# The output projection and the plain feed-forward in one block, at two stage borders

## What is computed

```
def squared_relu_mlp(h, w_up, w_down):
    return jnp.square(jax.nn.relu(h @ w_up)) @ w_down
...
        if layer % 2 == 0:
            x = x + gdn_shortconv_mixer(h, ev_w_in[i], ev_qkv_conv[i], ev_a_log[i], ev_dt_bias[i],
                                        ev_o_norm[i], ev_sc_conv[i], ev_w_out[i])
        else:
            x = x + nsa_mixer(h, od_w_in[i], od_cmp_pos[i], od_cmp_k_w1[i], od_cmp_k_w2[i],
                              od_cmp_v_w1[i], od_cmp_v_w2[i], od_w_out[i])
        x = x + squared_relu_mlp(rms_norm_2(x, mlp_norm[layer]), w_up[layer], w_down[layer])
    return rms_norm_2(x, final_norm)
```

## Time and profile before

| | us |
|---|---|
| median of 3 runs | 2354.27 |
| lowest, highest | 2346.55, 2355.38 |
| profiled execution | 2354.56 |
| its span | 2352.8 |
| TensorE busy | 2245.4 |
| VectorE busy | 986.6 |
| ScalarE busy | 752.9 |
| GpSimd busy | 193.3 |

### The profile page before, as it was taken

One profiled execution on the slowest core, in us unless ns is written; L12 is line 12 of the kernel. 1 busy time (PEld: TensorE's weight loads), 2 busy tenths in 40 slices (PEclk: granted clock), 3 DMA queues, 4 the chain that ended last, 5 costly groups with the idle time before them and its releaser, 6 DMA issues. The chain is left out here.

```text
span 2352.8 us, 30416 instructions
## 1 busy us (share of the span) xinstructions
PE 2245.4 (95%) x12790; PEld 1689.8 (72%) x12790; DVE 986.6 (42%) x1683; ACT 752.9 (32%) x1241; POOL 193.3 (8%) x214
## 2 busy tenths in 40 slices
PE   7999999889999999999999999999998999999997
PEld 4746555768888877874667888887875667888885
DVE  4123366443332334856344433423347653432433
ACT  3233211222222223444133322422125653331331
POOL 1004100000000000022000000000225540000000
PEclk9999999799999998999999999998999999999999
DMA  7240022212223112201031222213410012222210
GB/s 322 98 180 36 1 73 99 83 72 76 86 90 126 63 54 101 107 1 73 19 126 72 82 98 108 99 48 110 143 41 32 2 41 77 99 108 98 82 72 36
DMA packets 17110, 195.83 MB, mean 83 GB/s; under 512 B 2000, under 2 KB 3152, under 8 KB 5072
## 3 DMA queue, kind: packets, MB, share of 16 engines
q1 hardware_dynamic: 15824, 189.67, 21.7%
q10 hardware_dynamic: 1152, 4.23, 0.4%
HBM read 189.70 MB, written 2.10 MB: 82 GB/s over the span
## 5 line engine op out<-in xcount | busy, mean ns | idle before, releaser
L1733 DVE TENSOR_TENSOR wsp_mlp<-ring,wsp_mlp 128x1024 fp32r<-128x1024 f32 x128 | 156.8, 1225 | 438.0 <-ACT wsp_mlp L1695 438.0
L1695 ACT CAST wsp_mlp<-ring 128x1024 fp32r<-128x1024 f32 x128 | 134.3, 1049 | 349.2 <-PE psum L1680 344.8
L1677 PE MATMUL psum<-hs_mlp,wsp_mlp 128*128 128x512 f32 x512 | 201.7, 394 | 8.1 <-DVE hs_mlp L1566 8.1
L1677 PE MATMUL psum<-acts_mlp,wsp_mlp 128*128 128x512 f32 x512 | 202.4, 395 | 0.0
L1679 PE MATMUL psum<-hs_mlp,wsp_mlp 128*128 128x512 f32 x512 | 201.1, 393 | 0.0
L1680 PE MATMUL psum<-hs_mlp,wsp_mlp 128*128 128x512 f32 x512 | 201.1, 393 | 0.0
L1679 PE MATMUL psum<-acts_mlp,wsp_mlp 128*128 128x512 f32 x512 | 199.2, 389 | 0.0
L1680 PE MATMUL psum<-acts_mlp,wsp_mlp 128*128 128x512 f32 x512 | 199.2, 389 | 0.0
L1733 DVE TENSOR_TENSOR wsp_ffn<-ring,wsp_ffn 128x1024 fp32r<-128x1024 f32 x66 | 80.9, 1225 | 237.3 <-ACT wsp_ffn L1695 237.3
L1695 ACT CAST wsp_ffn<-ring 128x1024 fp32r<-128x1024 f32 x66 | 69.2, 1049 | 260.6 <-PE psum L1680 260.6
L1677 PE MATMUL psum<-hs_ffn,wsp_ffn 128*128 128x512 f32 x352 | 138.0, 392 | 8.4 <-DVE hs_ffn L1569 8.4
(11 more groups left out here) (460 smaller groups left out, 3905.3 us busy)
## 6 DMA issues: line engine op xcount, KB each, us to landing
ring<-weights SPq DMA_DIRECT2D x85, 2048.0 KB, 8.4
ring<-weights SPq DMA_DIRECT2D x3, 1024.0 KB, 4.8
xT<-xin SPq DMA_DIRECT2D x2, 1024.0 KB, 7.1
cst<-consts ACTq DMA_DIRECT2D x1, 1841.0 KB, 12.4
ring<-weights SPq DMA_DIRECT2D x1, 1280.0 KB, 5.5
mixT<-ctxin ACTq DMA_DIRECT2D x1, 1024.0 KB, 15.4
ring<-weights SPq DMA_DIRECT2D x2, 512.0 KB, 3.3
hT<-arena_low SPq DMA_DIRECT2D x8, 128.0 KB, 2.3
```

Of the source, the lines that this page charges most:

```text
L1677: pe.matmul(tile_bank(g, j), w_hi, src[:, 0, k0 + i, :], start=(first and i == 0), stop=False)
L1695: act.copy(wsp[:, q % 2, 0, :], raw_view(q)).then_inc(s["w_hi"], 1)
L1733: dve.tensor_tensor(wsp[:, q % 2, 1, :], raw_view(q), wsp[:, q % 2, 0, :].bitcast(F32), ALU.subtract).then_inc(s["w_lo"], 1)
```

## The change

For the two plain feed-forwards the projection's block is continued: `feed_forward` no longer opens a block but returns three functions, one for each compute engine, which the projection's block calls behind its own. The projection is told `follow=True` and leaves out its squares and ones-matmuls; it hands out `drain`, `square` and two waits, and the feed-forward, given it as `lead`, issues them. The gated feed-forward goes through `run_forward`, a block as before, with the old order.

For the feed-forward's tiles to be written while the projection runs, buffers are placed anew: the activations are two buffers, `act_hi` where the mixer's hT and mixT lay, `act_lo` over the projection's hs, the feed-forward's `hs` over the mixer's memory, and `wsp` at the projection's `wsp`. This holds for all three feed-forwards.

On TensorE the projection's units 6 and 7 come without ones-matmuls, then the feed-forward's unit 0, whose four output tiles each wait for the drain of the same bank; then four ones-matmuls, unit 1, four ones-matmuls, unit 2. The core of the diff:

```diff
-                for n in range(3, 8):
+                for n in range(3, 3 if follow else 8):
                     add_square(n)
...
+            def square(act, n):
+                act.wait_ge(x_set, base + n + 1)
+                act.activation(hT[:, n, :], xT[:, n, :], ACT.Square).then_inc(sq_set, 1)
...
+            act_hi = fsb("act_hi", [P, 16, T], F32R)
             hs = fsb("hs", [P, 2, KD, T], F32R)
-            acts = fsb("acts", [P, 2, 16, T], F32R)
-            wsp = fsb("wsp", [P, 2, 2, 1024], F32R)
             tmp = fsb("tmp", [P, 4, T], F32)
             rbc = fsb("rbc", [P, T], F32)
+            fsb("rest", [P, LOW1 - 2 * KD * T - 5 * T], F32)
+            act_lo = fsb("act_lo", [P, 16, T], F32R)
+            wsp = fsb("wsp", [P, 2, 2, 1024], F32R)
...
+                def lead_squares(first):
+                    for n in range(first, first + 4):
+                        lead.wait_square(pe, n + 1)
+                        pe.matmul(bank(sum0), C("ones"), lead.squares[:, n, :], start=(n == 0), stop=(n == 7))\
+                            .then_inc(s["lead_summed"], 1)
+
+                for q, (n, k, src, k0, first, last_k, g, ready) in enumerate(units):
+                    wait(pe, "w_lo", q + 1)
+                    if lead is not None and q in (1, 2):
+                        lead_squares(4 * q - 4)
...
+                    for j in range(4):
+                        if lead is not None and q == 0:
+                            lead.wait_x(pe, 5 + j)
...
+                    if q >= 2 or lead is not None:
+                        wait(act, "unit_done", q - 1)
+                    act.copy(wsp[:, q % 2, 0, :], raw_view(q)).then_inc(s["w_hi"], 1)
...
+                else:
+                    hidden_high(act, 0)
+                    hidden_high(act, 1)
+                    for n in range(4):
+                        lead.square(act, n)
+                        if n == 1:
+                            split(0)
+                    split(1)
+                    hidden_high(act, 2)
+                    hidden_high(act, 3)
+                    for n in range(4, 8):
+                        lead.square(act, n)
+                for q in range(NQ + 8):
+                    if lead is not None:
+                        if 1 <= q and q + 1 < NQ:
                             split(q + 1)
-                            hidden_high(act, q + 1)
-                        if q == 0 and shift is None:
+                        if q == 2:
                             root(act)
...
+                else:
+                    hidden_low(dve, 0)
+                    hidden_low(dve, 1)
+                    split(0)
+                    lead.drain(dve, 4)
+                    lead.drain(dve, 5)
+                    lead.drain(dve, 6)
+                    lead.drain(dve, 7)
+                    split(1)
+                    hidden_low(dve, 2)
+                    hidden_low(dve, 3)
```

More of the change, by code:

```diff
@@ L52 @@
 RING = 3
-Projection = namedtuple("Projection", "high low on_pe on_act on_dve")
+Projection = namedtuple("Projection", "high low on_pe on_act on_dve drain square wait_x wait_square squares")
+FeedForward = namedtuple("FeedForward", "on_pe on_act on_dve close")
 NEG = -1.0e30
@@ L1427, in program, with projection @@
         x_set, sq_set = sem("x_set"), sem("sq_set")
-        def projection(names, src, gate, hs, wsp, ready=None, order=(0, 1, 2, 3)):
+        def projection(names, src, gate, hs, wsp, ready=None, order=(0, 1, 2, 3), follow=False):
             sum_bank[0] = 0
@@ L1453, in on_act @@
                     high(act, q)
-                for q in range(13):
+                for q in range(7 if follow else 13):
                     if q + 1 >= begun:
                         high(act, q + 1)
[L1457 to L1460, removed]
+                    if q >= 5 and not follow:
+                        square(act, q - 5)
             def on_dve(dve, begun=0):
@@ L1464, in on_dve @@
                     low(dve, q)
-                for q in range(12):
+                for q in range(8 if follow else 12):
                     if q + 1 >= begun:
                         low(dve, q + 1)
[L1468 to L1479, removed]
+                    if q >= 4:
+                        drain(dve, q - 4)
+            return Projection(high, low, on_pe, on_act, on_dve, drain, square, wait_x, wait_square, hT)
         def project(names, src, gate):
@@ L1643, in place @@
                 return e - (sum(downs[0]) if part_of[e] else 0)
[L1645 to L1671, removed]
-                                    wait(pe, name, v)
-                        for j in range(4):
-                            for i in range(2):
-                                w_hi = wsp[:, q % 2, 0, i * 512 + j * P:i * 512 + (j + 1) * P]
-                                w_lo = wsp[:, q % 2, 1, i * 512 + j * P:i * 512 + (j + 1) * P]
-                                pe.matmul(tile_bank(g, j), w_hi, src[:, 0, k0 + i, :], start=(first and i == 0),
-                                          stop=False)
-                                pe.matmul(tile_bank(g, j), w_hi, src[:, 1, k0 + i, :], start=False, stop=False)
-                                last = pe.matmul(tile_bank(g, j), w_lo, src[:, 0, k0 + i, :], start=False,
-                                                 stop=(last_k and i == 1))
-                        last.then_inc(s["unit_done"], 1)
-                        if g == NG_ - 1 and q >= groups[NG_ - 2][1] + 3 and sq < 4:
-                            sq = add_square()
-                    while sq < 8:
-                        sq = add_square()
-                @block.scalar
-                def _(act):
-                    def split(q):
-                        i = raw[units[q][0]]
-                        act.wait_ge(weight_landed[i % RING], landed(i))
-                        if q >= 2:
-                            wait(act, "unit_done", q - 1)
-                        act.copy(wsp[:, q % 2, 0, :], raw_view(q)).then_inc(s["w_hi"], 1)
-                    if shift is not None:
-                        root(act)
@@ L2598, in program @@
         parts, hs, wsp = split_space("evo")
+        awaited = [signal for signal, _ in read_at[issued[0] - RING:]]
+        finished = [s_ for s_ in taken[delta_mixer:] if all(s_ is not a for a in awaited)]
         o_sq, o_sum, o_root, o_turned, o_inv, o_row, o_set, o_ready = (
@@ L2657, in _ @@
                 steps.on_dve(dve, begun=4)
+                mlp.on_dve(dve)
+            @block.gpsimd
+            def _(pool):
+                for s_ in finished:
+                    pool.sem_clear(s_)
             @block.sync
@@ L2956, in _ @@
                 odo.on_pe(pe)
+                mlp.on_pe(pe)
             @block.scalar
```

277 lines of the change are left out of this document (183 added, 94 removed).

## The result

The changed kernel is slower. Its median is 2363.3 us over seven runs (2362.86 to 2370.85), beside 2346.63 us for the kernel before over seven runs (2343.58 to 2357.15). The ratio is 1.0061, with a 95% interval of 1.0039 to 1.0082. The forecast was 2343.0 us with a range of 2336 to 2349.5, so the result lies above it.

A forecast was written before the change was run, and what follows sets the result against it. TensorE, busy 95% of the span, bounds the kernel, so time lay in its waits at two borders. Gains of 11.83 us, cut to 11.1 by the smaller clock term, from 2354.27 gave 2343 us, range 2336 to 2349.5.

The forecast's parts named there:

- The third rival: New buffer addresses slow TensorE in all three feed-forwards; from 2.2% worse pace the kernel takes 2366 us; chance 0.03.
- The border: Projection's unit 6 to feed-forward's unit 2: 29.74 us against 35.69 and 35.62, so 5.95 and 5.88 us gained.
- The wait: Feed-forward's unit 0 waits at the border for VectorE's drain 4 after the projection's unit 7: 1.02 us.
- The ones-matmuls: Eight per border, in two groups of four ahead of feed-forward units 1 and 2: 6.96 us together.
- What hides the moved work: Splits for unit 0 finish 2.7 us before the projection's unit 7 ends; later splits and the reciprocal also come in time.
- Rival 1: Clock falls at the new border wait too, slowing units 0 and 1 by 2.78 us per border: 2348.7 us; chance 0.12.
- Rival 2: Work ahead of unit 0 or 1 runs late, keeping a border wait of about 4 us: 2353.9 us; chance 0.08.
- The clock term: Slow clock after each border's old wait goes away: between 1.7 and 2.8 us per border, taken as 2.4.

The follow-up runs named there:

- e1: Changed kernel with all 232 words of filler moved ahead of act_hi, so all buffers begin at 192 modulo 256; 2344.35 us, ratio 0.9969.
- e5: Changed kernel with 104 words of the filler put ahead of act_hi, making the distance 0 modulo 256; 2345.51 us, ratio 0.9983.
- e8: Kernel before, its two blocks and order kept, with the changed kernel's buffer places and the filler ahead of act_hi; 2349.22 us, ratio 1.0004.
- e2: Kernel before, its two blocks and order kept, with the changed kernel's places for the feed-forward buffers; 2380.73 us, ratio 1.0119.
- e11: Kernel before run again without any edit, for its profile and clock; 2345.36 us, the lower group of its runs.
- e6: Changed kernel with 40 words of the filler put ahead of act_hi, making the distance 0 modulo 256; one run, 2339.56 us.
- e3: Changed kernel with 8 words of the filler put ahead of act_hi, making the distance 128 modulo 256; 2356.04 us, ratio 1.0025.
- e12: Kernel before with 24 words of unused filler ahead of wsp, so the weights begin 96 bytes further; 2387.65 us, ratio 1.0163.

## Why the prediction was wrong, point by point

**The step that failed** is one sentence: "Buffers get new addresses in all three feed-forwards; I cost that at nothing". Its reason was that the projections "with operands elsewhere" keep 5.44 a unit. They do, but there the moving operand and the weights are both at 192 modulo 256, so that row could not show the cost. What I compared were places; what counts is the distance between two buffers, which was 0 in every row that I had. The third rival named the loss of pace and its price (slower by 0.5% from 2.2% on, 2366 us), though not the distance; measured were 2.4 to 2.9%. Its 0.03 was the mistake, not its sum. The sum of it by units: 108 units on hs x 0.16 and 86 on activations x 0.13 are 28.5 us. With that the third rival's way of counting gives 2343 + 28.5 = 2371.5; that its 2366 lies so near the measured 2363.3 is luck, for after's clock (below) took the difference off.

That sum can be tested without the clock. A run's span times its mean granted clock is roughly what it would take at full clock throughout (waits are scaled too), and this number has a standard deviation of only 1 to 2 us from run to run:

| | runs | mean span | mean clock | at full clock |
|---|---|---|---|---|
| before, beside e1 and e5 | 38 | 2347.8 | 0.9745 | 2287.9 |
| e8, old order, distance 0 | 10 | 2348.4 | 0.9745 | 2288.5 |
| e1, new order, distance 0 | 10 | 2342.3 | 0.9747 | 2283.0 |
| e5, new order, distance 0 | 8 | 2341.6 | 0.9749 | 2282.8 |
| after | 7 | 2362.5 | 0.9786 | 2311.9 |
| e2, old order, after's layout | 4 | 2379.3 | 0.9730 | 2315.0 |

After less e1 is 28.9 us, e2 less before 27.1: the layout's cost, with either order. After's runs had a higher clock than before's (0.979 in six of seven), which hid 9.7 us of it: 0.0041 x 2362. In the profiles most of that is the borders, about 35 us each at 1.00 instead of 0.90, or 7 us in all.

**The border** was right term by term. With the distance mended, unit 6 to unit 2 is 29.40 us at both borders; I had 29.74. The wait was 0.88 for 1.02. The ones-matmuls read 3.03 (1243.74 to 1246.77), and the next slot 0.64 instead of 0.23, so 3.44 a group for 3.48. As the same 0.41 falls behind unit 2's start in the second group, the feed-forward's row is longer by about as much: 341.48 for 340.93, of which e8 (341.04) puts 0.11 on the new places. Set off against 35.69, which counts from the ones-matmul ahead of unit 6, the gain is 6.29 less 0.41, or 5.88 of the 5.95 foretold, in a profile where the border of before had its low clock.

**What hides the moved work** was right: VectorE stood idle ahead of drain 4, unit 1 waited for nothing, and the reciprocal (1257.10 + 3.36) was done 6.5 us before unit 4 needed it (1255.80 and two units of 5.6). **Rival 1**, a low clock at the new wait, did not come: the clock is 1.00 in every border row of the new order above. (Its sum has a slip: it puts 5.5 us of clock back where the forecast had counted 4.8, so its time would have been 2348.0.) **Rival 2**, a wait elsewhere, did not come.

**The clock term** is the open one. I took 2.4 us a border from it, 4.8 of the 11.1. At the borders it came. The time at 1.2 GHz by stage, in us, from the traces' records of the clock:

| profile | layer one | "evo" and feed-forward, layer two | mixer, layer three | from "odo" to the end | whole span |
|---|---|---|---|---|---|
| before, first | 44.7 | 11.7 | 27.3 | 15.0 | 131.0 |
| before, e11 | 28.4 | 11.3 | 27.3 | 15.0 | 110.6 |
| after | 27.9 | 4.7 | 27.3 | 8.2 | 97.0 |
| e1 | 44.8 | 5.4 | 30.1 | 8.7 | 121.4 |
| e5 | 31.7 | 3.9 | 30.2 | 8.8 | 100.9 |
| e6 | 28.4 | 5.3 | 36.8 | 8.7 | 107.7 |

Each border's stage has 6 to 8 us less at 1.2 GHz in all four profiles of the new order. In the plain means little is left of it: over all runs e1 and e5 have a mean clock of 0.9747 and 0.9749 against 0.9745, about 0.0003 x 2345, or 0.7 us. So the new order gains some 5 us at full clock (2287.9 less 2283.0 or 2282.8) and 0.7 of clock, 5.8 in the means, where I foretold 11.1. The runs show two reasons. In e1, e5 and e6 part of the low clock came back in layer three's mixer, which took 1.8 to 5.0 us longer than the 315.6 of before; in after and e3 it did not. In e6 the mixer and projection take 353.33 us where e11 has 348.84, at a clock of 0.95 for 0.96, for the same matmuls. And the means mix layer one's two lengths in unequal shares. The times of e1 and e5 have a gap of their own, at 2342 us: 11 of their 18 runs lie above it, where 13 of before's 38 lie above 2350. Group beside group the means are 2338.2 for 2346.4 and 2347.3 for 2355.5 us, so 8.2 us are gained in each. That sorting goes by the times; the two profiles among the 18 runs bear it out, e1's (2344.36 us) with the long layer one and e5's (2336.74) with the short one. Whether the unequal shares are chance isn't shown, and neither is why the mixer's clock fell in three profiles.

The Trainium skill ("TensorE: Matmul & The Clock Gate", section "What's actually happening") says that the gate runs freely, not from the kernel's start; the 417.03 and 410.54 us of the same work in two profiles of one kernel agree.

That e1's 2344.35 lies so near the forecast is luck too. The forecast began at 2354.27, the median of three runs of which two were of the upper group; from the 2348.48 beside e1 the same 11.1 us would have given 2337.4.

Loss and gain add up to the result: 28.9 us from the layout, 4.9 back from the order, and 9.7 back from the clock, on before's mean span of 2347.8, make 2362.1 where after has 2362.5.

## What to carry to other kernels

When buffers are moved, compare not where each lies but how far the moving operand and the weights lie from each other: here only a distance that was a multiple of 256 bytes kept the matmul's pace, and a line of filler in the wrong place cost 0.8% (after against e1) to 1.6% (e12). A pace that is the same in every row of a profile says nothing about a distance that is also the same in every row. And compare the clock stage by stage, in several runs: here the borders gave it back, while the plain mean of 18 runs hid that under two lengths of a stage that the change doesn't touch.

## What the hardware showed that I had not expected

An fp32r matmul of 128 x 512 takes a slot of 227 ns at full clock when the distance between its moving operand and its weights is a multiple of 256 bytes, and 229 to 235 ns, in the mean of a unit, at the distances of 64, 96, 128, 160 and 192 bytes, with TensorE busy throughout. The Trainium skill ("SBUF — State Buffer", section "Who interferes with whom") gives TensorE two independent read ports, one for the moving operand and one for the weight load, and has it wait for no one. By that the distance could not matter; e12's 352.18 against 340.93 us for the same matmuls says that it does, and the measurement decides. It is not the work of other engines, for the cost is the same where they and the DMA stand still (8.84 and 9.14 us for 39 slots). How TensorE's own accesses come to hinder each other isn't shown by these runs: no run changed the weight loads' timing.

Runs of the kernel before come in two lengths, about 9 us apart, and two profiles that show one of each differ mostly by the clock in layer one (8.6 of 9.2 us), with the same instructions.
